# Products that nothing reads, run by TensorE in seven waits of a hybrid decoder step

## The reference

```python
def run_trunk(x, pos, states, params, chunk):
    ...
        hdn = rmsnorm(x, ns[0])
        x = x + 0.5 * rmsnorm(swiglu(hdn, p['ffn_w_gate'][0], p['ffn_w_up'][0], p['ffn_w_down'][0]), ns[1])
        hdn = rmsnorm(x, ns[2])
        mix, st_new = token_mixers(hdn, pos, p, st, chunk)
        x = x + rmsnorm(mix, ns[3])
        hdn = rmsnorm(x, ns[4])
        x = x + 0.5 * rmsnorm(swiglu(hdn, p['ffn_w_gate'][1], p['ffn_w_up'][1], p['ffn_w_down'][1]), ns[5])
```

## Time and profile before

| | us |
|---|---|
| median of 3 runs | 1571.77 |
| the three runs | 1557.24, 1571.77, 1572.60 |
| the profiled execution: its time | 1556.96 |
| its span (first to last instruction) | 1555.1 |
| TensorE busy in the span | 1416.8 (91%) |
| VectorE, ScalarE, GpSimdE busy | 850.5, 583.3, 108.1 |
| mean granted TensorE clock | 0.923 of full speed |

### The profile page before, as it was taken

How to read it: one execution, slowest core, us unless ns; L and a number is a source line. 1 busy time by engine, 2 the same in 40 slices (tenths; PEclk the granted TensorE clock), 3 DMA queues, 4 the chain that set the end, 5 groups by cost and what they waited for, 6 DMA issues and landing times.

```text
span 1555.1 us, 28287 instructions
## 1 busy us (share of the span) xinstructions
PE 1416.8 (91%) x11544; PEld 1348.6 (87%) x11544; DVE 850.5 (55%) x1313; ACT 583.3 (38%) x837; POOL 108.1 (7%) x157
## 2 busy tenths in 40 slices
PE   5999997997898979999989999989979977999997
PEld 4899997987875979999979999888878766999995
DVE  4455448655334675554575554675543447655445
ACT  4333344642222443333443333446312325333342
POOL 5400000000020440000000000000000212000000
PEclk9999998999976789999989999989988857999997
DMA  7855443522311455554445554524122206455441
GB/s 200 193 163 162 149 160 99 163 82 82 96 32 30 56 158 167 166 171 134 146 136 162 162 159 148 180 82 134 57 83 70 44 18 127 136 162 162 156 161 40
DMA packets 205948, 193.86 MB, mean 125 GB/s; under 512 B 29380, under 2 KB 203924, under 8 KB 205728
## 3 DMA queue, kind: packets, MB, share of 16 engines
q1 hardware_dynamic: 200432, 184.50, 39.0%
q0 software_dynamic: 4496, 6.09, 2.5%
q10 hardware_dynamic: 928, 1.95, 0.4%
HBM read 186.32 MB, written 6.19 MB: 124 GB/s over the span
## 4 chain that ended last, share of the span: by engine, by line
PE 83%; DVE 7%; DMA 4%; ACT 3%; issue 2%; SPq 1%; ACTq 0%; DVEq 0%
PE ps L608 81%; DVE ring_r L1869 3%; PE ps L611 2%; DMA ring<-in_ffn_w_gate 2%; DMA ring<-in_ffn_w_up 1%; DMA big<-in_x_prompt 1%; SPq L564 1%; DVE y L1878 0%; ACT whigh_r L1434 0%; ACT L1448 0%; DVE x L1934 0%; DMA arena<-in_state_ret 0%; DVE big L2311 0%; DVE big L2310 0%; DVE XX L2138 0%
## 5 line engine op out<-in xcount | busy, mean ns | idle before, releaser
L1869 DVE TENSOR_TENSOR ring_r<-ring,whigh_r 128x2048 fp32r<-128x2048 f32 x168 | 376.3, 2240 | 356.6 <-ACT whigh_r L1434 356.6
L1434 ACT ACTIVATE whigh_r<-ring 128x2048 fp32r<-128x2048 f32 x168 | 314.4, 1872 | 352.0 <-PE ps L608 342.0
L608 PE MATMUL ps<-hdn,whigh_r 128*128 128x288 f32 x1920 | 328.7, 306 | 29.3 <-DVE ring_r L1869 29.3
L608 PE MATMUL ps<-hdn,ring_r 128*128 128x288 f32 x2016 | 353.0, 303 | 0.0
L608 PEld LDWEIGHTS ps<-hdn,whigh_r 128*128 128x128 f32 x1920 | 285.3, 195 | 33.1 <-issue 31.8
L608 PEld LDWEIGHTS ps<-hdn,ring_r 128*128 128x128 f32 x2016 | 308.4, 197 | 0.0
L608 PE MATMUL ps<-y_r,whigh_r 128*128 128x288 f32 x1792 | 275.8, 298 | 0.0
L608 PEld LDWEIGHTS ps<-y_r,whigh_r 128*128 128x128 f32 x1792 | 252.8, 190 | 0.0
L608 PE MATMUL ps<-big_r,whigh_r 128*128 128x288 f32 x832 | 137.0, 300 | 8.2 <-DVE arena_r L1869 8.2
L608 PEld LDWEIGHTS ps<-big_r,whigh_r 128*128 128x128 f32 x832 | 119.7, 191 | 9.9 <-issue 9.2
L608 PE MATMUL ps<-big_r,ring_r 128*128 128x288 f32 x704 | 110.7, 298 | 0.0
(11 more groups left out here) (424 smaller groups left out, 1340.8 us busy)
## 6 DMA issues: line engine op xcount, KB each, us to landing
ring<-in_ffn_w_gate SPq DMA_DIRECT2D x44, 1024.0 KB, 5.4
ring<-in_ffn_w_up SPq DMA_DIRECT2D x44, 1024.0 KB, 5.4
ring<-in_ffn_w_down SPq DMA_DIRECT2D x32, 1024.0 KB, 5.0
ring<-in_w_in SPq DMA_DIRECT2D x30, 1024.0 KB, 5.3
ring<-in_ffn_w_down SPq DMA_DIRECT2D x16, 768.0 KB, 4.3
ring<-in_w_out SPq DMA_DIRECT2D x8, 1024.0 KB, 5.2
cst<-in_const POOLq DMA_DIRECT2D x1, 1953.5 KB, 10.0
big<-in_x_prompt ACTq DMA_DIRECT2D x2, 512.0 KB, 9.2
```

The costliest lines, as they stand in the source:

```text
L608: return pe.matmul(out, lhsT, rhs, start=start, stop=stop, **k)
L1434: A(high(pos)[:, 0:rows * 256], ring[:, s, 0:rows * 256], ACT.Copy)\
L1869: return TT(out, in_, high, ALU.subtract)
```

## The change

TensorE gets products whose results nobody reads. `keep_busy` runs 28 products of 288 columns into bank 7 behind each of the five `norm_sums` between two stages, from the rounded part of the next stage's first weight block; it first waits until that is written. `busy_mask` runs products of 128 columns with an identity as both operands: 36 into bank 2 ahead of the wait for the first divided tokens at the end of the mixing stage, and 16 into bank 3 ahead of the wait for the divided sample tokens. The wait for `out_root` of `ssd` (bank 2 has been read) now also stands ahead of the 36. Nothing else moves.

```diff
+            def keep_busy(l, pos, n):
+                hold(sem("weights_high"), l * N_POS + pos + 1)
+                for _ in range(n):
+                    mm(ps[:, 7, 0:T], high(pos)[:, 0:P], high(pos)[:, P:P + T])
...
+                def busy_mask(bank, n):
+                    for _ in range(n):
+                        mm(ps[:, bank, 0:P], identR, identR)
...
                 after("probs_ready", "ml", 2)
                 state("ml", 1, 5)
+                after("out_root", "ssd")
+                busy_mask(2, 36)
                 after("raw_made", "ml", 0)
                 out("ml", 2, 1)
                 weights_sum(2, 7)
...
                 after("out_root", "ssd")
                 sample_add("ml")
+                busy_mask(3, 16)
                 after("raw_made", "ml", 2)
                 sums("ml", (1, 7))
                 slot_ready(l, POS_OUT)
...
                 ffn(l, 0)
                 norm_sums(l, 0)
+                keep_busy(l, POS_IN, 28)
                 mixers(l)
...
                 hold(sem("last_read"), l + 1)
                 norm_sums(l, 1)
+                keep_busy(l, POS_FFN[1], 28)
                 ffn(l, 1)
                 norm_sums(l, 2)
+                if l + 1 < DEPTH:
+                    keep_busy(l + 1, 0, 28)
```

## The result

The changed kernel takes 1576.72 us (median of 12 runs, 1569.79 to 1591.17), the kernel before 1561.66 us in as many runs beside it (1551.91 to 1580.87): ratio 1.0100, interval [1.0057, 1.0143]. The means differ by 14.1 us (8 to 20 by resampling the runs). So the change makes the kernel slower by about 1%, at the edge of what was called telling, and outside the interval of no difference. The prediction said 1569 and "no change", on a median of three runs that lay 10 us above that of twelve.

What follows compares the result with a forecast made beforehand. TensorE's work in order was taken to bound the kernel (83% of the chain of waits). 2 x (2.8 + 1.2) - 2.9 = +5.1 us on 1556.96 gave 1562.1, or 1576.9 at the high level: 1569 between them, range 1547 to 1582.

Steps and rivals of the forecast that it cites:

- The masks' price: End of mixing, each layer: 36 products at 211 ns overrun their wait, +2.8 us; 16 more delay the sums, +1.2 us.
- keep_busy's -2.9 us: Five places between stages: full clock through the first wait gains 5.9 us together or nothing; half was taken.
- The cover: First wait between stages: the rounded weight block is ready 10 us ahead, so keep_busy costs nothing; otherwise 2.6 us a place.
- the level: Whole kernel: runs lie low or high with the same chance, 1562.1 or 1576.9 us for the median, 1569 between them.
- The mask lifts the clock: End of mixing: the mask products raise the clock; -10.5 us in all, 1546.5 or 1561.3 us; chance 0.28.
- Nothing but the places: End of mixing: the waits hide both masks, leaving only the gain between stages, -2.9 us: 1554.1 or 1568.9; chance 0.15.
- The loads are not hidden: End of mixing: unhidden weight loads make a mask product 313 ns at 0.50; +15.9 us, 1572.9 or 1587.6; chance 0.09.
- (1): Sign at the five places between stages: 28 new products right behind the sums, tile 0 still some 4.3 us after them.
- (4): Sign at the end of mixing: 36 products 211 ns apart at 0.50, sample products some 7.6 us behind the state, not 4.76.
- (5): Sign at the end of mixing: 3.4 us of mask products ahead of the sums.
- (2): Sign between stages: a clock of 1.00 through the first wait, then a fall between tile 1 and tile 3.
- (3): Sign between stages: the first low-half product comes between 9.1 and 9.6 us after tile 2.

Runs made afterwards that it cites:

- e3_short_masks: Kernel before plus half the masks, 18 and 8 narrow products instead of 36 and 16, no keep_busy: 1560.70 us, ratio 0.9984.
- e10_double_masks: Kernel before plus twice the masks, 72 and 32 narrow products, no keep_busy: 1591.93 us, ratio 1.0206 in 6 runs.
- e2_keep_only: Changed kernel without its masks and the moved wait, keep_busy at all five places: 1566.89 us, ratio 1.0044 to the kernel before.
- e4: Kernel before plus masks of 18 and 8 products that stream 288 columns, no keep_busy: 1552.86 us, ratio 0.9961.
- e7: Changed kernel with 18 and 8 masks of 288 columns and 20 more products ahead of tile 2: 1552.20 us, ratio 0.9931 to the kernel before.
- e8: Changed kernel with 18 and 8 masks of 288 columns in place of the narrow ones: 1559.37 us, ratio 0.9934 to the kernel before.
- e9: Kernel before with an empty diff, timed against itself: 1558.29 us, ratio 0.9998.
- e11: Kernel before plus keep_busy at all five places and 20 products ahead of tile 2, no masks: 1548.95 us, ratio 0.9948.
- e1: Changed kernel without keep_busy, the 36 and 16 narrow masks kept: 1577.97 us, ratio 1.0080 to the kernel before.
- e5: Kernel before plus keep_busy only at the two places ahead of the mixing stages, no masks: 1566.28 us, ratio 1.0013.
- e6: Kernel before plus keep_busy only at the three places ahead of feed-forward parts, no masks: 1567.31 us, ratio 1.0045.
- e12: Kernel before plus only the 20 products ahead of tile 2, no keep_busy, no masks: 1569.68 us, ratio 1.0049.
- e13: Kernel before plus 20 products ahead of tile 2 and 18 and 8 masks of 288 columns, no keep_busy: 1555.32 us, ratio 0.9971.

## Why the prediction was wrong, point by point

**The masks' price** was right. 211 ns a product forecast, 213 to 216 measured; +2.8 and +1.2 us a layer forecast, +3.04 and +1.29 measured, in both layers; the clock stayed at 0.50. `e3_short_masks` shows that products inside the wait are free, `e10_double_masks` that the price scales. The Trainium skill's load time (TensorE: Matmul & The Clock Gate, LDWEIGHTS), one figure with no clock named, by which this term would have been 0, was rightly set aside at this clock.

**The step that failed first is keep_busy's -2.9 us.** Its frame held: hidden, clock 1.00 in the first wait at A, C and D, a fall between tile 1 and tile 3, VectorE's pace as the next limit. What failed is "I take half": the low stretch behind tile 2 lasted as long as before (4.85 us against 4.40 at A), the first low-half product came 9.67 us after tile 2 where 9.1 to 9.6 were forecast, and the places' sum rose from 94.5 to 95.0 us. What decided was how long the clock stays low behind the second wait. In the 20 places with keep_busy and an empty second wait it stayed low for 6.8 us in 16 and for 3.4 us in 4. In those four the first low-half product came 9.03 us after tile 2, as the prediction had it for the short case; but the mean over all 20 is 9.61 us, and 9.60 in the 35 without filler. The value was the named end, 0, where -2.9 was added up. The bound of 5.9 us itself held: with both waits filled the places gave 6.1 and 5.7. The prediction had said that the second wait "stays uncovered", and had the row that 2.16 us of waiting were enough at E; it should have given that row more weight than the half.

The cover was a little thinner than said, too. The rounded block itself was 10 us ahead, as read. But the load of that block lands late in some launches and holds up the sums, which come 9.1 us after its rounding begins (9.5 once) in all 15 profiles. After such a wait the sums run at 0.50, and so do the first of the 28 products. `e2_keep_only` at B:

```profile
558.76 1.33 PE L608 MATMUL ps<-ssum,cst 128*128 128x288 f32 x2 [6.29 <-DVE ssum L1919]
559.88 2.27 PE L608 MATMUL ps<-er,cst 128*128 128x288 f32 x4
561.54 5.55 PE L608 MATMUL ps<-big_r 128*128 128x288 f32 x28
566.93 0.29 PE L608 MATMUL ps<-hdn,big_r 128*128 128x288 f32 x1
```

Tile 0 comes 8.17 us after the sum, in place of 7.65, with no wait left: 0.5 us late, and taken back in the wait ahead of tile 2 (4.40 us from tile 0 to tile 2 in place of 4.91), as forecast.

**The second step that failed is the level.** The sum was +5.1 us, but it was placed "between two levels" 15 us apart, at 1569: below the shown median of 1571.77. So the forecast pointed down, while the measured median rose by 1.0%. There are no two levels. In 116 runs of the kernel before on four chips the time runs from 1547 to 1580 with one peak, mean 1561.4, and follows the mean granted clock of the run (correlation -0.91, 14.7 us for each 0.01). Three runs and a profile cannot place such a median; the sum should have been put on the median as it stood.

**The sum.** +9.2 us are seen in place (8.7 from the ends, 0.5 from the places), +14.1 (8 to 20) were measured. The 5 us between are inside the interval, and are not settled. The same comparison for the other kernels (means less what ends and places show) gives -2.4 to +2.0 for `e3`, `e4`, `e7`, `e8`, `e9`, `e10` and `e11`, but +5.7 to +9.8 for `e1`, `e2`, `e5`, `e6`, `e12` and `e13`, more often than chance gives. (By the ratios the excess of `e1`, `e5` and `e13` is 4 to 5 us, and `e8` comes out 7 us under.)

The granted clocks of the runs say what kind of time that is. A run's span times (1 - its mean clock) is what it loses to the low clock. For `e2` this is 5.8 us less than for the runs beside it, while its profile has 13.9 less in the places and ends (against the mean of the two profiles of the kernel before). So 8.1 us more were lost elsewhere, and the time elsewhere was 8.0 us longer. In all six kernels it is so: 5.4 to 10.9 us more lost elsewhere, 4.6 to 9.3 us longer there. A longer wait would not do that, as at 0.50 only half of its length counts as lost. The excess is time at 0.50 outside the places and ends. Most such time lies in the mixing stages (35 to 65 us in a profile, against 9 to 17 in the feed-forward parts together). Over all profiles a mixing stage behind keep_busy with an empty second wait took 231.9 us (8 stages, 221 to 235), one behind no filler 227.5 (14 stages, 221 to 234). That is a hint for `e2` and `e5`, within the scatter, and none for `e1`, `e6`, `e12` and `e13`. What makes the clock fall there more often stays open.

**The rivals.** *The mask lifts the clock*: not with these products; `e4_wide_masks` has it with wider ones. *Nothing but the places*: no, the masks cost 8.7. *The loads are not hidden*: no, 213 and not 313 ns. What decided about keep_busy was no rival of mine but a clause of the forecast, the second wait, at too small a weight.

**The signs.** (1), (4) and (5) came as described, (2) at A, C and D. (3) did not: the first low-half product came 9.64 to 10.14 us after tile 2.

## What to carry to other kernels

Before filling a wait to keep the clock, list all the waits behind it up to the work that is to gain, and fill them all: here the first alone shortened nothing on the mean and both gave 6 us in place. The second wait came from VectorE's order, a 2.28 us split ahead of tile 2; moving that split was not tried. Filler is free only while it ends inside the wait at the clock that is granted there; take its price at the low level, here 213 ns and not 114. Of the two kinds of filler tried at the end of mixing, the one with 288 streamed columns for each load was followed by a rise of the clock in all eight stages and the one with 128 in none: try the wide one first. And read the scatter of the runs against their granted clock before trusting a median of three.

## What the runs showed of the hardware

- At 0.50, products of 128 weight columns and 128 streamed ones follow each other every 213 ns (211 had been worked out from the earlier trace rows, and 114 at 1.00), and those with 288 streamed columns every 240: two and a quarter times the columns for an eighth more time.
- 72 narrow products in a row, 15.6 us with no gap, left the granted clock at 0.50; with 18 products of 288 columns, 4.7 us long in the same place, it rose 2.4 to 5.7 us after their start. The Trainium skill (TensorE: Matmul & The Clock Gate, part 1) says that sustained matmul activity releases the throttle; the trace agrees for the wide products and not for the narrow ones.
- A launch's time follows its mean granted clock (-0.91 over 116 runs), and the same stage of the same work took 220.5 to 235.0 us.
- The load of the first gate block at E is issued as the mixing stage ends, among the stores of the states; from 1308 to 1328 us of the change's profile the loads took 51% of the DMA engines' time and the stores 29%. From its issue to ScalarE's start it took 15.0 us before the change (1283.91 to 1298.88) and 19.6 us after (1308.60 to 1328.19); with nothing changed it was 19.0 us in `e9_unchanged` (1273.96 to 1292.91). Over all 15 profiles it was 12.7 to 22.2 us, 14.8 with the most masks (`e10_double_masks`) and 22.2 with none (`e12_second_only`). The scatter is of the launch, not of the change:

```profile
1328.19 1.91 ACT L1450 ACTIVATE big_r<-ring 128x2048 fp32r<-128x2048 f32 x1 [8.06 <-DMA ring<-in_ffn_w_gate]
1337.28 1.33 PE L608 MATMUL ps<-ssum,cst 128*128 128x288 f32 x2 [8.55 <-DVE ssum L1922]
```
